# Both source tables of V on GpSimd, the second half first, with a scratch of their own

## The reference

```python
bb_re = coef_re[..., None] * br - coef_im[..., None] * bi
bb_im = coef_re[..., None] * bi + coef_im[..., None] * br
bu_re = jnp.einsum('blgc,gpc->blgp', uf, bb_re)
bu_im = jnp.einsum('blgc,gpc->blgp', uf, bb_im)
...
_, _, xr, xi = lax.associative_scan(combine, (a_re_t, a_im_t, bu_re, bu_im), axis=1)
```

## Time and profile before

| | |
|---|---|
| median of 3 runs | 742.48 us (741.82 to 744.68) |
| the profiled execution | 742.09 us |
| its span, first to last instruction | 740.3 us |
| mean granted TensorE clock | 0.979 |
| busy share of the span | PE 94%, PEld 74%, DVE 63%, ACT 42%, POOL 42% |
| chain that ended last, by engine | PE 77%, DVE 10%, POOL 5%, ACT 3% |

### The profile page before, as it was taken

How to read it: one execution, slowest core, us unless ns; L and a number is a source line. 1 busy time by engine, 2 the same in 40 slices (tenths; PEclk the granted TensorE clock), 3 DMA queues, 4 the chain that set the end, 5 groups by cost and what they waited for, 6 DMA issues and landing times.

```text
span 740.3 us, 9867 instructions
## 1 busy us (share of the span) xinstructions
PE 694.1 (94%) x3566; PEld 550.4 (74%) x3566; DVE 468.9 (63%) x796; ACT 310.9 (42%) x488; POOL 310.7 (42%) x242
## 2 busy tenths in 40 slices
PE   0799999998979889999999999999999999999997
PEld 0587777787755566778898888888878887888886
DVE  2878987998977688778856787655564555000005
ACT  4445346836624556613775434434434344112110
POOL 2001899509957399000005344244343353343340
PEclk9899999999988989999999999999999999999999
DMA  9953131261068470925813322332322313313303
GB/s 330 390 132 86 58 114 58 71 175 40 1 72 156 153 290 17 380 95 192 320 54 110 113 88 83 113 97 73 113 83 88 113 62 109 113 59 112 114 1 114
DMA packets 63081, 91.47 MB, mean 124 GB/s; under 512 B 12010, under 2 KB 41474, under 8 KB 62979
## 3 DMA queue, kind: packets, MB, share of 16 engines
q1 hardware_dynamic: 59520, 89.44, 37.6%
q10 hardware_dynamic: 3523, 1.54, 0.9%
HBM read 86.28 MB, written 4.69 MB: 123 GB/s over the span
## 4 chain that ended last, share of the span: by engine, by line
PE 77%; DVE 10%; POOL 5%; ACT 3%; issue 2%; DMA 1%; SPq 0%; ACTq 0%; DVEq 0%; POOLq 0%
PE bank L1665 22%; PE bank L1667 21%; PE bank L1666 21%; PE bank L1670 3%; PE bank L1900 2%; PE bank L2015 1%; DVE arena L1213 1%; DVE arena L1238 1%; DMA xh<-in_x 1%; DVE w_lo L1223 1%; PE bank L1880 1%; PE bank L2010 1%; PE bank L1992 1%; PE bank L1675 1%; PE bank L2033 1%
## 5 line engine op out<-in xcount | busy, mean ns | idle before, releaser
L512 POOL TENSOR_TENSOR w_lo<-w_raw,w_hi 128x2048 fp32r<-128x2048 f32 x32 | 147.7, 4617 | 285.9 <-ACT w_hi L1104 227.4
L1665 PE MATMUL bank<-act_hi,w_hi 128*128 128x512 f32 (+1 forms) x384 | 145.3, 378 | 0.1
L1667 PE MATMUL bank<-act_hi,w_lo 128*128 128x512 f32 (+1 forms) x384 | 144.3, 376 | 0.0
L1666 PE MATMUL bank<-act_lo,w_hi 128*128 128x512 f32 (+1 forms) x384 | 144.3, 376 | 0.0
L1665 PE MATMUL bank<-w_hi,act_hi 128*128 128x512 f32 x240 | 100.4, 418 | 0.3 <-DVE act_lo L1264 0.3
L1667 PE MATMUL bank<-w_hi,act_lo 128*128 128x512 f32 x240 | 96.2, 401 | 0.0
L1666 PE MATMUL bank<-w_lo,act_hi 128*128 128x512 f32 x240 | 96.2, 401 | 0.0
L747 ACT ACTIVATE w_hi<-w_raw 128x2048 fp32r<-128x2048 f32 x26 | 49.8, 1914 | 94.4 <-PE bank L1667 90.8
L1665 PEld LDWEIGHTS bank<-act_hi,w_hi 128*128 128x128 f32 x384 | 72.3, 188 | 14.6 <-DVE conv L1621 0.3
L1666 PEld LDWEIGHTS bank<-act_lo,w_hi 128*128 128x128 f32 x384 | 72.4, 188 | 14.3 <-issue 0.2
L1667 PEld LDWEIGHTS bank<-act_hi,w_lo 128*128 128x128 f32 x384 | 72.3, 188 | 14.1
(11 more groups left out here) (324 smaller groups left out, 1178.4 us busy)
## 6 DMA issues: line engine op xcount, KB each, us to landing
w_raw<-in_w_up SPq DMA_DIRECT2D x44, 512.0 KB, 4.7
arena<-in_w_ada SPq DMA_DIRECT2D x16, 1024.0 KB, 10.6
w_raw<-in_w_down SPq DMA_DIRECT2D x22, 512.0 KB, 3.9
w_raw<-in_w_in SPq DMA_DIRECT2D x10, 1024.0 KB, 5.1
xh<-in_x SPq DMA_DIRECT2D x8, 512.0 KB, 5.2
w_raw<-in_w_out SPq DMA_DIRECT2D x4, 1024.0 KB, 12.1
arena<-in_w_ada SPq DMA_DIRECT2D x2, 2048.0 KB, 11.1
arena<-lag_dram SPq DMA_DIRECT2D x16, 128.0 KB, 5.4
```

Source lines behind the costliest of these rows:

```text
L512: nc.gpsimd.tensor_tensor(w_lo[:, slot, 0:width], w_raw[:, slot, 0:width], w_hi[:, slot, 0:width].bitcast(F32), ALU.subtract).then_inc(S[" ...
L1665: T.matmul(dst, lhs_hi, rhs_hi, start=start, stop=False)
L1666: T.matmul(dst, lhs_hi, rhs_lo, start=False, stop=False)
L1667: return T.matmul(dst, lhs_lo, rhs_hi, start=False, stop=stop)
```

## The change

POOL makes both halves. It starts half 1 right behind `future(3)`, once all square sums are done (`sq_used` 8, since the table lies where the squares were); then it waits for `vt_ready` 1 and for `rot_ready` 9 (all queries rotated, since half 0 lies where the raw queries were) and makes half 0. DVE's call is gone. PE's turns of half 0 wait for `vt_ready` 2, those of half 1 for 1. The scratch is no longer `up32` but 1024 columns of the arena that held the indexer's low parts until the last score.

```diff
@@ -202,7 +202,7 @@
-        vt_part = up32[:].rearrange("p a n -> p (a n)")
+        vt_part = cut(6656, 1024)
@@ -665,10 +665,13 @@
             future(3)
             pool.wait_ge(S["turn_ready"], 1)
-            pool.wait_ge(S["vt_ready"], 1)
+            pool.wait_ge(S["sq_used"], 2 * TT)
             for part in range(3):
                 source_of_v(G, link, 1, part)
+            pool.wait_ge(S["vt_ready"], 1)
             pool.wait_ge(S["rot_ready"], 9)
+            for part in range(3):
+                source_of_v(G, link, 0, part)
             pool.wait_ge(S["turned_ready"], 13)
             pool.wait_ge(S["vt_ready"], 2)
@@ -1417,9 +1420,6 @@
             link(V.tensor_scalar(q_scale, rstd_qk[:, 32:64], -ATT_SCALE, None, ALU.mult))
-            dve.wait_ge(S["s5_bb_ready"], 1)
-            for part in range(3):
-                source_of_v(V, link, 0, part)
@@ -1949,7 +1949,7 @@
-                        pe.wait_ge(S["vt_ready"], half + 1)
+                        pe.wait_ge(S["vt_ready"], 2 - half)
```

## The result

The changed kernel took **751.61 us** (median of 10 runs), the kernel before 742.23 (also 10). The ratio of the two is 1.0140, 95% interval 1.0111 to 1.0169, that is **+10.4 us** (8.2 to 12.5); the two medians by themselves are 9.4 apart. The profiled execution of the changed kernel took 754.84 us with a span of 753.0, 12.7 longer than the span before.

A forecast was written before the change was run, and what follows sets the result against it. It took POOL's chain, 3.58 us late at PE's lags of half 1, and the two `lo` of U_V as what matters. 9.1 + 2.6 - 3.8 + 0.6 = +8.5 us on 742.1 gave 750.6, range 743.9 to 754.4.

The forecast's parts named there:

- rival A: POOL's six half 1 instructions alternate with DVE's before `lo(U_V)`, making it 11.7 us late; total 750.6 us; chance 0.70.
- Rival B: POOL gets turns only where DVE waits on its own result; four of six precede `lo(U_V)`; 746.5 us; chance 0.16.
- rival C: No clash to speak of at the rotations, lags of half 1 warm, its scan 3.8 us earlier; 738.3 us; chance 0.07.
- rival D: PE's wait for `lo(U_V)` hidden, DVE's net loss of 4.4 us taken by its idle time; 742.1 us; chance 0.07.
- PE's wait and the clock: At the U_V products: PE idle 9.1 us for `lo(U_V)`, then 2.6 us lost to the lower clock.
- DVE's 7.3 us saved: Half 0's table leaving DVE saves it 7.3 us, worth nothing, as its next need is PE's logits of units 4 and 5.
- What gets given back, −3.8: At the scan of half 1: DVE's 3.8 us wait for PE's states is used up, so the scan starts 7.9 us late.
- PE regains 3.6 + 2.6 at the lags: At PE's lags of half 1: the 3.58 us idle time and the 2.6 us of cold lags are gone.
- no wait of DVE L1459 for PE's states: Expected sign in the changed profile: DVE no longer waits for PE's states, a wait of 3.8 us before.
- The 0.6 us of a longer cold stretch ahead of `y`: PE idles about 2 us longer ahead of `y`, and the cold stretch behind it costs 0.6 us.

The follow-up runs named there:

- e6: Changed kernel with only the first two POOL instructions of half 1 beside the rotations, the other four after both `lo` of U_V; ratio 1.0058 to the kernel before.
- e2: Changed kernel with half 1's six table instructions replaced by 14 POOL memsets, which read nothing; ratio 0.9977 to the kernel before.
- e1: Changed kernel with POOL starting half 1 only after both `lo` of U_V are ready; ratio 1.0046 to the kernel before.
- e3: Kernel before with POOL's table of half 1 left out, two memsets in its place; ratio 1.0025 to the kernel before.
- e7: Kernel before with only two top-k rounds moved from unit 10 to unit 13; ratio 1.0001.
- e5: Kernel before with part 0 of half 1 made early on POOL ahead of `future(3)`, two top-k rounds moved from unit 10 to 13; ratio 0.9970.
- e9: The kernel of e5, but the two top-k rounds moved behind the scan of half 1 (units 14 and 15); ratio 0.9968 to the kernel before.
- e4: Four POOL instructions of half 1 before `future(3)`, the last two after both `lo`, seven top-k rounds moved ahead; ratio 1.0063 to the kernel before.
- e8: The kernel of e5 run again unchanged; ratio 1.0000 to the kernel before.

## Why the prediction was right, and where it was not

The forecast was +8.5 on the profiled execution, 750.6 us, with a median nearer 751; measured were a median of 751.61, +10.4 (8.2 to 12.5) by the ratio, and +12.7 on the profiled execution. The sign and the mechanism of the loss hold. One step was wrong, and its error was partly covered by others; that the forecast came so near is in part luck.

**The clash, rival A: right.** The instructions came in turn, one of DVE's between any two of POOL's. `lo(U_V)` ended at 162.60 and not at 151.1: 11.5 late (forecast 11.7). POOL's half 1 ended at 159.8 as forecast, half 0 at 182.07 (182.3). In the small, e6 shows the same (two for two), and e2 that it takes POOL's reads. Rival B fell with the six held instructions ahead of `lo(U_V)`, rival C with their times, rival D with PE's wait.

**PE's wait and the clock: right, a little too large.** 8.7 us against 9.1 and 1.9 against 2.6. I had taken the loss of the cold lags for that of the cold products; the products lost less. The sentence ahead of it, that the clock is at its lower level after an idle time like the one of 3.58 us, is not a rule: behind 8.68 us it was 0.50, but behind 3.58 us in e1 it was 1.00.

**DVE's 7.3 us saved: worth nothing, right.** It waited 5.75 us for the first logits instead of 0.24. These, and not the logits of units 4 and 5, were the next thing that DVE needed from PE, and from there on DVE was as late as PE.

**What gets given back, −3.8: the step that failed.** It began with "PE regains 3.6 + 2.6 at the lags", and before that: "PE's idle 3.58 us and its cold lags are gone". I had read the wait ahead of the lags of half 1 off its one named releaser, POOL's L550. The code has two that end late:

```python
1987                    pe.wait_ge(S["lag_w_ready"], half + 1)
1989                    pe.wait_ge(*((S["u_t_read"], 2), (S["state_read"], 1))[half])
```

The second is raised by DVE's L1462 in the scan of half 0, and in the kernel before it fell only 0.3 us ahead of POOL's. My own step had all of DVE's work up to this scan 11.7 us late; so `state_read` was late by it, the lags with it, PE's states behind the lags with them, and DVE's wait for these states, which I wanted to use up, stayed at 3.94 us: "no wait of DVE L1459 for PE's states", one of the signs that I had named, did not come. e3 shows it in the kernel before, with POOL 11 us early and no gain, e7 from the other side, and the changed profile in PE's 4.03 us.

The same mistake was in rival C: POOL's L550 ended only about 0.3 us behind DVE's L1462, so about that much could be regained at the lags and not 3.8. e2, without a clash, came out near the kernel before.

**The 0.6 us of a longer cold stretch ahead of `y`: not seen.** C to D is 15.37 against 15.28.

**The sum as it was.** 8.7 + 1.9 from the clash, nothing given back: 10.6 of the 10.8 in A to B, and the measured +10.4. The forecast's 11.7 − 3.8 + 0.6 came near because the first term was 1.1 too large and the 0.6 didn't come either: together they made up for 1.7 of the 3.8 that never came. That is luck, not insight.

**The last 1.7 us of the profiled execution** (B to C) are probably not the change's. 1.5 of them are at the first logits: there PE stands idle for 0.9 and then 0.5 us (1.3 in e5 and e9) in every trace, and the clock behind it falls to its lower level in some traces and stays full in others. In the changed kernel's it fell (0.50 at 182 us, above). In the kernel before it stayed:

```profile
170.00:172.00 2.00, 2.00 (x9) 1.00 0.03 8
```

From PE's first logits to DVE's of unit 4 it is 14.1 us in before, e1, e3 and e6, where the clock stayed at 1.00, and 15.6 in the changed kernel, e2, e4 and e7, where it fell to 0.50. In e5, e8 and e9, with the longer second wait, it fell each time. Only one kernel has two traces, e5 and e8, and it fell in both, so that it changes from one execution to the next of one kernel isn't shown; among the first eight it follows no edit that I can name. Without it the profiled 12.7 would be 11.2, within the interval of the ratio.

## What to carry to other kernels

Before idle time of GpSimd is filled, look at what VectorE runs in that window: each GpSimd instruction that reads SBUF is to be priced as a full-length stop of VectorE's next instruction with two SBUF inputs, or next `tensor_scalar` within SBUF, however small that one is (with the stop they took 2.0 to 2.8 us each here), and the sum compared with the cover of what VectorE makes for TensorE (2.6 us here). And before a wait is counted as gained, look up every semaphore that the waiting instruction needs and when each came: the profile names the last, and here the next was 0.3 us behind it on the other engine. A stall with two causes falls only when both are moved: as in e5 and e9, where it shrank to less than 1 us, and not in e3 or e7.

## What the runs showed of the hardware that was not expected

A two-input instruction of 32 columns, 0.19 us alone, took 2.06 and 2.29 us beside POOL (e4). And instructions with a single tensor input were held as well, two of int32 in e4 (1.96 us each, above) and DVE's L1422 in the changed kernel:

```profile
169.05 2.02 DVE L1422 TENSOR_SCALAR stat<-stat 128x32 f32<-128x32 f32 x1
```

The same line took 0.17 us in e6 and 0.18 before the change (there L1419). Here it ended with POOL's L336 of half 0, at 171.0. The Trainium skill, in the section named under e2, counts `tensor_scalar` among the operations that can take both of the ports and so contend; these rows agree, with 2.02 and 1.96 us. Whether forms with one input other than `tensor_scalar` collide was not tried.

The length of an idle time did not decide the clock behind it. Behind 0.9 and 0.5 us it fell in four of eight traces (the changed kernel, e2, e4, e7) and stayed full in four (before, e1, e3, e6), which costs 1.5 us in the attention loop. Behind the 0.85 us ahead of e6's product it stayed full too. Behind 3.58 us ahead of the lags it was 0.50 in the kernel before and 1.00 in e1, and the same 32 products took 6.24 and 3.68 us; behind the 2.14 us in e6 they took 5.19.
